# Two-block model on one core: a new order for the second block's projections, levels beside the output gate, first convolution tap on ACT

## What is computed

```python
n = rms_norm(x, attn_norm_g)
(g_qkv, g_lr, g_out, nq, kc, vc, ks, vs, kw, vw, ng) = split(n @ w_in)
g_qkv = silu(causal_short_conv(g_qkv, gla_conv_w))      # 4 taps per channel
gq, gk, gv = split(g_qkv)                               # 512, 512, 1024 channels
log_a = log_sigmoid(g_lr @ gate_w2 + gate_b) / 16       # decay per key channel
# gated linear attention: 4 heads, causal, scores weighted by exp(sums of log_a)
gla = rms_norm(o, norm_g) * silu(g_out)
# second mixer: 8 query heads, keys and values compressed, selected and in a window
cmp = silu(blocks(kc, vc) + pos @ w1) @ w2
h = x + concat(gla, nsa) @ w_out
out = h + (silu(m @ w_gate) * (m @ w_up)) @ w_down      # m = rms_norm(h)
```

## Time and profile before

| | us |
|---|---|
| median of 3 runs (2772.37 to 2774.28) | 2773.87 |
| the profiled execution | 2771.57 |
| its span in the trace | 2769.6 |
| PE busy | 2698.8 (97%) |
| ACT, POOL, DVE busy | 1229.6, 1182.9, 1134.2 |

### The profile page before, as it was taken

The page is one execution under the profiler, slowest core; times in us unless marked ns, Lnnn a source line. Parts: engine busy times, 40 slices in busy tenths (PEclk is TensorE's granted clock), DMA queues, the critical chain, the costliest instruction groups (busy, mean ns, idle before and its releaser), DMA issues.

```text
span 2769.6 us, 33895 instructions
## 1 busy us (share of the span) xinstructions
PE 2698.8 (97%) x13864; PEld 2300.0 (83%) x13864; DVE 1134.2 (41%) x1363; ACT 1229.6 (44%) x1501; POOL 1182.9 (43%) x536
## 2 busy tenths in 40 slices
PE   8999999999999999999999978999999999999999
PEld 8998877778888888888888877988788888888887
DVE  6777744433432322223323477346432222222222
ACT  6434444444444444444444444535454444444333
POOL 3555653344444444444444334332244444444443
PEclk9999999999999999999999999999999999999999
DMA  6444444355555555555555532453355555555554
GB/s 235 168 157 150 158 150 163 134 207 188 186 189 188 186 194 184 196 183 201 188 199 190 178 122 106 168 184 124 122 184 192 187 193 185 191 188 196 196 200 152
DMA packets 72441, 489.00 MB, mean 177 GB/s; under 512 B 8363, under 2 KB 10060, under 8 KB 14688
## 3 DMA queue, kind: packets, MB, share of 16 engines
q1 hardware_dynamic: 72288, 486.84, 50.0%
HBM read 484.71 MB, written 2.10 MB: 176 GB/s over the span
## 4 chain that ended last, share of the span: by engine, by line
PE 88%; DVE 6%; issue 2%; ACT 2%; POOL 1%; DMA 0%; DVEq 0%; ACTq 0%; SPq 0%; POOLq 0%
PE PB L572 24%; PE PB L576 24%; PE PB L573 24%; PE PB L540 3%; PE PB L544 3%; PE PB L541 3%; PE PB L590 1%; DVE TM L2333 1%; ACT WH L1099 1%; DVE WL L1620 1%; POOL WL L2423 1%; DVE TM L2330 1%; PE PB L669 0%; PE PB L691 0%; PE PB L1064 0%
## 5 line engine op out<-in xcount | busy, mean ns | idle before, releaser
L2423 POOL TENSOR_TENSOR WL<-RAW,WH 128x1024 fp32r<-128x1024 f32 x442 | 1076.2, 2435 | 1473.5 <-ACT WH L1099 1473.4
L1099 ACT ACTIVATE WH<-RAW 128x1024 fp32r<-128x1024 f32 x892 | 940.0, 1058 | 1171.2 <-PE PB L576 1105.6
L1620 DVE TENSOR_TENSOR WL<-RAW,WH 128x1024 fp32r<-128x1024 f32 x450 | 581.4, 1293 | 1479.4 <-ACT WH L1099 1479.1
L572 PE MATMUL PB<-WH,HNH 128*128 128x512 f32 x1888 | 742.0, 393 | 5.0 <-DVE MIX L2268 4.6
L576 PE MATMUL PB<-WL,HNH 128*128 128x512 f32 x1888 | 736.6, 390 | 2.3 <-POOL WL L2423 2.2
L573 PE MATMUL PB<-WH,HNL 128*128 128x512 f32 x1888 | 736.3, 390 | 0.0
L572 PEld LDWEIGHTS PB<-WH,HNH 128*128 128x128 f32 x1888 | 355.5, 188 | 82.4 <-DVE MIX L2268 5.8
L576 PEld LDWEIGHTS PB<-WL,HNH 128*128 128x128 f32 x1888 | 355.3, 188 | 77.4 <-POOL WL L2423 3.1
L573 PEld LDWEIGHTS PB<-WH,HNL 128*128 128x128 f32 x1888 | 355.5, 188 | 72.3
L540 PE MATMUL PB<-HNH,WH 128*128 128x256 f32 x1184 | 347.9, 294 | 9.7 <-ACT WH L1099 9.7
L544 PE MATMUL PB<-HNH,WL 128*128 128x256 f32 x1184 | 340.1, 287 | 9.9 <-POOL WL L2423 6.0
(11 more groups left out here) (343 smaller groups left out, 2076.9 us busy)
## 6 DMA issues: line engine op xcount, KB each, us to landing
RAW<-in_w_gu SPq DMA_DIRECT2D x176, 1024.0 KB, 4.8
RAW<-in_w_dn SPq DMA_DIRECT2D x88, 1024.0 KB, 4.8
RAW<-in_w_in_a SPq DMA_DIRECT2D x57, 1024.0 KB, 4.8
RAW<-in_w_in SPq DMA_DIRECT2D x45, 1024.0 KB, 4.8
RAW<-in_w_out SPq DMA_DIRECT2D x32, 1024.0 KB, 4.8
RAW<-in_w_ga SPq DMA_DIRECT2D x24, 1024.0 KB, 4.8
RAW<-in_w_gb SPq DMA_DIRECT2D x24, 1024.0 KB, 4.8
WIN<-in_win SPq DMA_DIRECT2D x8, 512.0 KB, 5.7
```

Source lines behind the costliest of these rows:

```text
L572: e.matmul(o, hi[:, k, x], WH[:, s, c], start=k == 0, stop=False)
L1099: e.activation(WH[:, u % NSPL, :], RAW[:, n % NRAW, half * SU * 128:(half + 1) * SU * 128], ACT.Copy).then_inc(*wt.act.mark(("wh", u)))
L1620: e.tensor_tensor(WL[:, u % NSPL, :], RAW[:, n % NRAW, half * SU * 128:(half + 1) * SU * 128], f32(WH[:, u % NSPL, :]), ALU.subtract).then ...
L2423: e.tensor_tensor(WL[:, u % NSPL, :], RAW[:, n % NRAW, half * SU * 128:(half + 1) * SU * 128], f32(WH[:, u % NSPL, :]), ALU.subtract).then ...
```

## The change

1. SECOND, NT and the weights' order in HBM: after lr come og, ks, kc, then v, vs; before it was v, og, ks, kc, vs. All else keeps its place.
2. The side generators `gla` and `nsa` become four parts, `levels`, `keys`, `outputs`, `heads`, called by `second`: levels at 1.3/16, then all at 3.4/16: keys after (ks, 3), "cb" after them, then outputs after (v, 7) and 8 idle steps, then heads after (cmp, 1). PE does level 0 at its step 6, not 5. A fourth buffer GE3 is added, and `before`, `after` and `taken` reach back four levels, not three.
3. The first tap is an ACT copy with a scale (`conv_first`); DVE does only the scaling at a row's end and the three taps one row later (`conv_next`, `conv4`). The Silus come two rows after the row. Rows c0 to c2 are no longer convolved in one piece.
4. CB moves to the place of GE0 and GE1, the small third norm gets NB2; `keys` waits for level 7 on PE where it waited for the end of `outputs`. v_turned 6 and 7 move from og to vs. In the diff, `nsa`'s helper functions on DVE are otherwise only moved outward.

```diff
-        GE = [ar("GE0", [128, 4, T], 32), ar("GE1", [128, 4, T], 36), GG]
+        GE = [ar("GE0", [128, 4, T], 32), ar("GE1", [128, 4, T], 36), GG, ar("GE3", [128, 4, T], 76)]
...
-        SECOND = (("v", 8, 16), ("og", 2, 64), ("ks", 4, 16), ("kc", 4, 16), ("vs", 1, 64),
+        SECOND = (("og", 2, 64), ("ks", 4, 16), ("kc", 4, 16), ("v", 8, 16), ("vs", 1, 64),
                   ("cmp", 2, 32), ("nq", 8, 16), ("mg", 4, 32))
...
+        def second(w, levels, keys, outputs, heads):
+
+            yield from levels
+            w.rate = 3.4 / 16.0
             yield from passed(w, "ks", 3)
-            for _ in range(4):
-                yield
+            yield from keys
+            w.passed.add("cb")
+            yield from passed(w, "v", 7)
+            yield from idle(8)
+            yield from outputs
+            yield from passed(w, "cmp", 1)
+            yield from heads
...
-            def gla():
+            def levels():
...
+                yield from idle(4)
                 for lv in range(8):
-                    x = GE[lv % 3]
+                    x = GE[lv % 4]
...
                                          start=True, stop=True)
                     t.then_inc(*gl.pe.mark(("level", lv)))
                     yield
-                yield
+
+            def outputs():
                 for h in range(4):
-                    yield from passed(w, "og", h // 2)
...
-                        group(nt, HNH, HNL, 16)
+                        group(nt, HNH, HNL, 16, None, {1: values_turned})
                     elif name == "og":
-                        group(NT["og"] + 2 * j, HNH, HNL, 16, None, {} if j else {1: values_turned, 2: gates_turned})
+                        group(NT["og"] + 2 * j, HNH, HNL, 16, None, {} if j else {2: gates_turned})
...
-                        tile_row(nt, 16, None, {8: lambda: v_turned(j - 2)} if name == "v" and j > 1 else {})
+                        tile_row(nt, 16, None, {9: lambda: v_turned(j - 2)} if name == "v" and j > 1 else {})
...
                 e.activation(ge, ge, ACT.Exp, scale=-1.0).then_inc(*gl.act.mark("exp"))
@@ -1225,7 +1225,7 @@
                 yield
                 yield
                 for lv in range(8):
-                    ge = GE[lv % 3]
+                    ge = GE[lv % 4]
...
-                yield
-                yield
+                yield from idle(3)
                 e.wait_ge(*gl.pe.done("level", 7))
                 e.activation(flat(PT2[:, :, :]), bank("level", 7, 0)[:, :],
                              ACT.Copy).then_inc(*gl.act.mark("pt2", frees("level", 7, 0)))
                 yield
...
+            def conv_first(j):
+
+                e.wait_ge(*m.dve.done("cs4", j))
+                if 2 <= j < 10:
+                    e.wait_ge(*m.act.done("c", j - 2))
+                if j >= 10:
+                    e.wait_ge(*m.pe.done("v", j - 10))
+                e.activation(TM[:, (2 * j + 1) % 4, :], TM[:, 2 * j % 4, :], ACT.Copy, scale=vec("gw3", j)).then_inc(
+                    *m.act.mark(("c4", j)))
+
+            taps = {(2, 12): (0,), (3, 3): (1,), (3, 11): (2,), **{(j + 1, 2): (j,) for j in range(3, 8)}}
+            silus = {(3, 5): (0,), (3, 13): (1,), (4, 4): (2,), **{(j + 2, 4): (j,) for j in range(3, 7)}, (8, 12): (7,)}
+
             def conv_silu(j):
                 e.wait_ge(*m.dve.done("c", j))
...
-                    if j > 3 and k == 1:
-                        conv_silu(j - 1)
-                if j == 2:
-                    for p in range(3):
+                    for p in taps.get((j, k), ()):
+                        conv_first(p)
+                    for p in silus.get((j, k), ()):
                         conv_silu(p)
...
-                        if k == 1 and (name == "v" and j or name == "og" and j == 0):
-                            p = (j - 1) % 8
-                            e.wait_ge(*m.dve.done("c", 8 + p))
-                            x = TM[:, (2 * p + 1) % 4, :]
-                            e.activation(x, x, ACT.Silu).then_inc(*m.act.mark(("v", p)))
+                        if k == 2 and (name == "v" and j or name == "vs"):
+                            conv_first(8 + (j - 1) % 8)
+                        if k == 4 and (name == "v" and j > 1 or name == "vs"):
+                            value_silu((j - 2) % 8)
+                        if k == 10 and name == "vs":
+                            value_silu(7)
...
                 def before(lv):
 
-                    if lv >= 3:
-                        e.wait_ge(*gl.pe.done("level", lv - 3))
+                    if lv >= 4:
+                        e.wait_ge(*gl.pe.done("level", lv - 4))
                     e.wait_ge(*d.done("gb"))
-                    ge = GE[lv % 3]
...
                 for lv in range(1, 8):
                     keys(lv - 1)
                     before(lv)
-                    if lv >= 3:
-                        taken(lv - 3)
+                    if lv >= 4:
+                        taken(lv - 4)
                     yield
                 keys(7)
-                taken(5)
-                yield
-                taken(6)
-                yield
-                yield
+                for lv in range(4, 7):
+                    taken(lv)
+                    yield
+                yield
...
                 for i, gain in enumerate(("ksg", "kwg", "kcg")):
...
                 yield
                 yield from passed(w, "kc", 3)
                 e.wait_ge(landed["pos"], 16)
+                e.wait_ge(*gl.pe.done("level", 7))
                 e.wait_ge(*m.dve.done("kc", 1, 1))
...
-                w.passed.add("cb")
-                yield
-                yield from passed(w, "cmp", 1)
+                yield
+
+            def heads():
+                d = ns.dve
...
-            def conv4(nt, j, freed):
+            def conv4(j):
+
                 s, y = TM[:, 2 * j % 4, :], TM[:, (2 * j + 1) % 4, :]
-                scaled(nt, s, freed)
-                e.wait_ge(*m.dve.prev())
-                if 2 <= j < 10:
-                    e.wait_ge(*m.act.done("c", j - 2))
-                if j >= 10:
-                    e.wait_ge(*m.pe.done("v", j - 10))
-                e.tensor_scalar(y, s, vec("gw3", j), None, ALU.mult).then_inc(*m.dve.mark())
+                e.wait_ge(*m.act.done("c4", j))
                 for i in range(1, 4):
-                    e.wait_ge(*m.dve.prev())
+                    if i > 1:
+                        e.wait_ge(*m.dve.prev())
                     e.scalar_tensor_tensor(out=y[:, i:T], in0=s[:, 0:T - i], scalar=vec(f"gw{3 - i}", j),
                                            in1=y[:, i:T], op0=ALU.mult, op1=ALU.add).then_inc(
                                                *m.dve.mark(*([("c", j)] if i == 3 else [])))
 
+            def conv_next(first, j):
+
+                if j % 8:
+                    conv4(j - 1)
+                nt = first + j % 8
+                scaled(nt, TM[:, 2 * j % 4, :], [("cs4", j), ("free", nt)])
+
+            scalings = {(2, 9): (0,), (2, 16): (1,), (3, 9): (2,), **{(j, 16): (j,) for j in range(3, 8)}}
...
-                if j == 2:
-                    for i in range(3):
-                        conv4(NT["c"] + i, i, [("free", NT["c"] + i)])
-                elif 2 < j < 8:
-                    conv4(nt, j, [("free", nt)])
+                    for p in scalings.get((j, k), ()):
+                        conv_next(NT["c"], p)
+                    if j == 8 and k == 8:
+                        conv4(7)
+                for p in scalings.get((j, 16), ()):
+                    conv_next(NT["c"], p)
                 if j == 8:
                     scaled(nt, TM[:, 0, :], [("lr"), ("free", nt)])
-            w.beside(second(w, gla(), nsa()), 1.3)
+            w.beside(second(w, levels(), keys(), outputs(), heads()), 1.3)
 
...
-                        if name == "v" and j > 1 and k == 12:
+                        if name == "v" and j > 1 and k == 13:
                             v_turned(j - 2)
-                        if name == "og" and j == 0 and k in (22, 24):
-                            v_turned(6 if k == 22 else 7)
+                        if name == "vs" and k == 6:
+                            conv4(15)
+                        if name == "vs" and k in (24, 26):
+                            v_turned(6 if k == 24 else 7)
...
-                        conv4(nt, 8 + j, [("free", nt)])
+                        conv_next(NT["v"], 8 + j)
...
                 queries(7)
-                yield
-                yield
-                yield
-                for h in range(4):
-                    yield from passed(w, "og", h // 2)
-                    yield
-                for _ in range(6):
-                    yield
+                yield from idle(4)
```

More of the change, by code:

```diff
@@ L371, in nsa_steps @@
                     yield from passed(w, "nq", h + 1)
-                    yield
-                    yield
-                for _ in range(4):
-                    yield
+                    yield from idle(2)
```

(44 more changed lines are left out.)

178 lines of the change are left out of this document (82 added, 96 removed).

## The result

The changed kernel takes **2776.6 us** in the median (2774.2 to 2779.7), the kernel before 2772.3 in the same session: a ratio of **1.0016 [1.0009, 1.0022]**. That is 4.4 us more, where 17 us less was predicted, and above the range of 2743 to 2770. The profiled execution took 2779.3 us with a span of 2777.0 (before: 2769.6).

What follows compares the result with a forecast made beforehand. PE's 27.0 us of waits before level 7, mostly naming DVE, and the clock were taken as the limit; 20.7 - 2.0 - 1.6 = 17.1 us off the 2773.9 median gave 2756.8, range 2743 to 2770.

Steps and rivals of the forecast that it cites:

- Part 1: Group c and LR: first tap to ACT, convolutions later; loop 5.2 us a row, lr's row ending at 1608.1.
- its lag: ACT's tap waits for DVE's scaling with the next cast queued behind: 0.5 us of 8.2 allowed, costing nothing.
- the backlog: End of group c: LR's copy, some 7 us after its row's matmuls, would lose that delay; LR ready at T = 1.1.
- Part 2: Output gate and keys under the levels: chain bound until level 4 at T = 70.6, level 7 at 1698.6 against 1717.5.
- Part 2's later step of PE: Levels: matmul-to-copy distance stays, bank wait stays possible; first level gains 4 us of slack, removing most of 8.5.
- The 16.8 us of waits: PE's remaining waits until level 4, at WL, WH and L800: chain at T = 70.6, PE without waits at 53.8.
- Part 3: Behind level 7: 113.0 + 0.5 us to the compression against 115.3; then 2.0 for mg and 1.6 of waiting.
- The first: Rival, levels: the chain fits PE's 6.2 us a step, 17 us of waits and 1.6 go too: 2738; chance 0.10.
- The third: Rival, levels: DVE and POOL lock each other, 22 us, 2779; decided by q above 2.2 or k above 1.5; chance 0.08.
- The fourth: Rival, value rows: the convolution loop moves there, 7.0 us a row instead of 6.0, about 2765; chance 0.10.
- The second: Rival: clock and new waits take half the gain, half speed doubling 8 us in the PE-bound end: 2765 to 2768; chance 0.20.
- The fifth: Rival: waits only shift (27 to 25), group c's clean part is kept, outputs eat it: 2770; chance 0.07.

Runs made afterwards that it cites:

- the earlier step: Changed kernel with PE's extra empty step and PE's levels one step earlier, as before the change, all engines at 14 steps: 1.0023 of the kernel before.
- the levels' low halves: Changed kernel with the low halves of the 18 weight units under the levels all on DVE, where every second was on POOL: 0.9974 of the kernel before.

## Why the prediction was wrong

- **Part 1, the step that failed.** It gave DVE 1.03 us of relief for each first tap, summed the new loop of group c from durations (taps 1.52) and got 5.2 us; it is 7.17. ACT's tap, 0.51 for the 0.45 that I took, has almost no part in that. The three taps' 1.52 was read from a row in which POOL had nothing to do (1577.79; its low halves there start at 1567.59 and 1580.79), and it is 1.52 in the later rows too only because the first tap takes the wait. Taking that tap away did not take the wait for POOL away, it passed it on. Predicted for LR -8.9 us, measured +0.8. The rule that speaks against it was on the table: by the Trainium skill (SBUF — State Buffer, Who interferes with whom) a DVE instruction with two SBUF inputs and a GpSimd one that reads SBUF lock each other out. I asked it only of keys and queries in the levels, not of the taps. The trace agrees with it, 3.66 against 1.52 us.
- **The same Part 1, its lag.** "0.5 us after the row, of 8.2 allowed: nothing" held for the value rows: 113.3 us, PE's wait there 0.8.
- **Part 1, the backlog.** "DVE's backlog goes with it" failed with the loop. PE's row of lr ended at 1613.7, but LR was ready at 1623.2, at T = 9.5 by the prediction's count and not at 1.1.
- **Part 2, mostly right.** Counted from LR (ready at T = 1.1 in the prediction, so that T = 0 is 1622.1 here), the low half behind the scans was done at T = 22.4 (22.5 predicted), level 4 began at T = 74.5 (70.6), level 7 at T = 93.5 (90.5). The 16.8 us of waits came as 19.2: 10.7 for OG, 4.7 for weights, 3.8 for PT; 1.2 for LR came on top, where none was predicted. But the wait for the eviction of OG was not in the list by itself: the chain was priced as one sum, and who stands in whose queue was not asked for ACT's evictions. The stretch's own gain was 6.9 of 10.0.
- **Part 2's later step of PE** was worth 11 us, against "the bank wait stays possible; the first level gains 4 us of slack".
- **Part 3, right.** 113.3 against 113.0 + 0.5. CB took 6.08 us and no PE wait came behind it. The mg transposes waited 2.2 (1.6 predicted), the stretch grew by 4.4 (3.6).
- **The heads, not looked at.** They had no term in the sum. Their 7.4 us came from a count that can be made in the diff: 13 yields on one engine, 14 on the others, and a rate that changes behind them. One empty step took 8.5 us off the stretch. That is the second step that failed.
- **The rivals.** The first (everything hidden) did not come: 19.2 us of waits stayed under the levels. The third had the mechanism, and its point of decision was reached: DVE's keys rose to 1.60 us in the mean. But level 7 came 3 us later than forecast, counted from LR, and not 22; the lock's cost fell in group c. The fourth (the value rows' loop) did not come: it is what the order without the convolution's split pays. The second (clock) had its part in the heads, behind waits that it did not name. The fifth's time, 2770, was the nearest, for another reason.

Left open: why PE ran slower with the earlier step, beyond what the clock shows, and how the 9 us of the levels' low halves divide between their length and the hold-ups.

## What to carry to other kernels

Look at the spread of an instruction before its mean is used: a form with 0.35 us at the least and 2.05 at the most was waiting for another engine inside its duration here, and when it was removed its neighbour waited instead. Where engines walk a shared order in steps of their own, count the steps of each, and the rate behind them, after every edit. And a swap that is right where a loop is the limit can be wrong in the next stage, where lag is.

## What the runs showed of the hardware

- A DVE instruction with a single tensor in SBUF and a scalar by partition (TENSOR_SCALAR, 128x256) is held up by POOL like one with two: 2.04 us against 0.35, until POOL's low half had ended. POOL lost at most 0.1 us by it: 2.49, where its low half takes 2.40 in the median of the whole kernel. By the Trainium skill (SBUF — State Buffer, Who interferes with whom), this form can enter a mode that takes the shared port pair, and whoever issues first keeps it for the whole instruction; start times and ends agree with that here.
- DVE's scaling, with one input in PSUM and one in SBUF, stayed at 0.42 us under the same low half (1590.78 in the kernel before).
- Moving a low half from POOL (2.5 us) to an already busy DVE (1.2 us) made both kernels 9 to 12 us faster, while DVE's work grew.
- The Silu behind a table load starts 1.29 us after the load does, and the Exp too (1664.13, 1647.70), and the load starts as the instruction before it ends (1662.84): the drain of about 1.38 us that the Trainium skill (ScalarE: Activation LUTs, What ACT_TABLE_LOAD costs) adds to it is not seen in these rows, as the prediction had it.
